# The down projection of a decoder's feed-forward layer as seven block products, its operands streamed through a ring of four slots

## The chip, the cores and the metric

The kernel runs on one core of a Trainium2 chip. The metric is the time of one execution on the device in microseconds (us), lower is better; three executions of the kernel before are given by their median. A core has five engines that run side by side, each with its own queue of instructions in program order: TensorE (PE, matrix products into the accumulators in PSUM, with its weight loads as PEld), VectorE (DVE), ScalarE (ACT), GpSimd (POOL) and SyncE (SP), which here only issues DMAs. They wait for one another through semaphores.

## The reference

One inference step of a decoder layer in float32: normalise, project, four groups of heads, output projection, then the feed-forward part that the change touches. The prompt has 1024 positions, the samples add 8, so each matrix of activations has 1032 columns when it lies transposed (features on the partitions).

```python
def conv_ffn(x, g, w_up, conv_w, conv_b, w_down, buf):
    t = x.shape[1]
    up = rmsnorm(x, g) @ w_up
    ext = jnp.concatenate([buf.astype(up.dtype), up], axis=1)
    conv = conv_b + sum(ext[:, i:i + t] * conv_w[i] for i in range(CONV_W))
    a, gate = jnp.split(conv, 2, axis=-1)
    y = (jax.nn.silu(gate) * a) @ w_down
    return y, ext[:, t:]
...
xp = xp + f.astype(xp.dtype)
```

`D_MODEL` is 1024, `D_FF` is 2816 (22 tiles of 128 features). `w_down` is 2816 x 1024: its product with the gated activations, added to the residual x, is the last stage of the kernel and the subject of this case.

## The kernel before, in words

Three things are common to all large products here. First, a float32 operand is split into a high part, which ACT makes by a copy to the type float32r, and a low part, which DVE makes by subtracting the high part from the raw value. Second, a product is three matmuls: high by high, high by low, low by high. Third, one stationary block of 128x128 weights meets some hundred columns of activations.

**The up projection** (line 1338 on, `seven`) runs in 22 passes p, one for each pair of a value tile and its gate tile. Each pass is a 2x2 block product by Winograd's scheme: seven block products P1 to P7 for eight, on sums of activations (T1 to T4) and of weights (S1 to S4), each product with 4 tiles of depth, 2 column parts of 258 and 3 matmuls per part: 168 matmuls of 258 columns in a pass. Behind it DVE and ACT put the pieces together, run the convolution over positions (`affine`, `taps`), `silu` and `gated`, and SP stores the gated tile of 1032 columns to DRAM (`scr_act`, `act_store`). `NPROD` is 154, the number of these products.

**The down projection** (PE lines 1401 to 1432, `down`) is a plain product. `GRAN` cuts it into 24 granules: a group of output tiles d and a range of depth tiles f. SP loads a granule's weights (`down_load`, line 857) into one of two buffers `dnr` when the granule two before is done, ACT splits them (`down_hi`, line 1900), DVE too (`down_low`, line 2750). The 22 tiles of activations are loaded back from DRAM once (`act_loads`, line 864), split once (ACT line 1766, DVE line 2598 by `act_hi`, `act_low`) and stay in SBUF as `fh`, `fl`, `hhi`, `hlo`. For each of the 8 output tiles d there are 22 f, 3 column parts of 344 and 3 matmuls: 8 x 22 x 3 x 3 = 1584 matmuls of 344 columns. Two sets of three PSUM banks take turns by d, so DVE adds the residual to a finished tile d (`add_y`, line 2824) while PE fills the other set. GpSimd loads the residual into `yst` and stores the sum. The last tile d is added and stored in three parts (line 2835, SP line 900).

The order on every engine is written out by hand; there is no scheduler. Line 1418 is the only wait of PE on the adds:

```python
if dd[0] >= 2 and fa_ == 0:
    pe.wait_ge(S("x2_add"), KC + dd[0] - 1)
```

Of the kernel before, what the change touches and what calls it, by code (L numbers as in the profile page):

```python
# [98 lines left out]
def build(nc, t):  # L99
# [5 lines left out]
    with ctx:  # L105
# [161 lines left out]
        fh = []  # L267
        for n, o5 in ((0, Q), (1, Q + 8256), (2, set0), (3, set0 + 8256), (4, Q + 16512), (5, Q + 24768), (6, Q + 33024),
                      (7, Q + 41280), (12, set1), (13, set1 + 8256), (14, set1 + 16512), (19, conv0), (20, conv0 + 8256),
                      (21, base)):  # L270
            h_, o6 = at(f"fh{n}", [P, COLS], f32r, o5)
            fh.append((n, h_[:, :], at(f"fl{n}", [P, COLS], f32r, o6)[0][:, :], at(f"fr{n}", [P, COLS], f32, o6)[0][:, :]))
        fh = {n: (h_, l_, r_) for n, h_, l_, r_ in fh}
        for j in range(KC):
            fh[8 + j if j < 4 else 11 + j] = (hhi[:, j, :], hlo[:, j, :], hlr[:, j, :])
        dst2 = [spare, set0 + 16512]
        dnh, dnl, dnr = [], [], []
        for n in range(2):
            h_, o6 = at(f"dnh{n}", [P, 1024], f32r, dst2[n])
            dnh.append(h_)  # L280
            dnl.append(at(f"dnl{n}", [P, 1024], f32r, o6)[0])
            dnr.append(at(f"dnr{n}", [P, 1024], f32, o6)[0])
        yst = at("yst", [P, COLS], f32, base + 8256)[0]
# [192 lines left out]
        g_end = {d: max(n for n in range(NG) if d in GRAN[n][0]) for d in range(KC)}  # L476
# [65 lines left out]
        def k_total(n):  # L542
            return 64 * (n // 4 + 1) if n < NKA else 64 * (NKA // 4) + 16 * ((n - NKA) // 4 + 1)
        SET_END = {}
# [13 lines left out]
        def _(sp):  # L558
# [2441 lines left out]
```

## Time and profile before

| what | value |
|---|---|
| median of three runs | 1352.65 us (1349.96 to 1356.93) |
| span of the profiled execution, first to last instruction | 1348.4 us |
| the same execution's own time | not recorded; the median lies 4.25 us above the span |
| PE busy | 1302.1 us (97%) |
| DVE busy | 946.2 us (70%) |
| ACT busy | 555.1 us (41%) |
| down projection, first product to the end of the last | 1092.8 to 1345.6 us |

The span is what the instructions cover; the time of a run has a few microseconds more around it. "Busy" of PE includes overlap: matmuls are pipelined, so one that lasts 0.28 us starts 0.12 us after the one before, and it is the distance of the starts that adds up. In a timeline a bracket at the row's end gives the idle time of the engine before it and what released it. PEclk is the clock that was granted to TensorE as a share of 2.4 GHz: 0.50 is 1.2 GHz.

### The profile page before, as it was taken

How to read it: one execution, taken by the hardware profiler on the slowest of the kernel's cores; microseconds unless marked ns; L12 is line 12 of the kernel's file. 1: busy time of each engine (PE TensorE's matmuls, PEld its weight loads, DVE VectorE, ACT ScalarE, POOL GpSimd, SP SyncE). 2: the span in 40 equal slices, each digit the busy share in tenths (PEclk: the TensorE clock that was granted, in tenths of full speed). 3: DMA queues.
4: the chain of work that ended last, by engine and by line, in shares of the span. 5: the costliest groups of instructions: out<-in, count | busy, mean ns of one | idle time of the engine just before them, and what ended most of it. 6: DMA issues, size and time to landing. Idle time of an engine off the chain costs nothing.

```text
span 1348.4 us, 24281 instructions
## 1 busy us (share of the span) xinstructions
PE 1302.1 (97%) x9271; PEld 1198.1 (89%) x9271; DVE 946.2 (70%) x1390; ACT 555.1 (41%) x913; POOL 217.1 (16%) x222
## 2 busy tenths in 40 slices
PE   7999999989989999999999999999999999999999
PEld 5888787767667678899999999999999998999999
DVE  6678889988898767567697888887788894211111
ACT  6623111355567665343545435445445463000100
POOL 0420034323333430100201101101101000000000
PEclk9999999979999999999999999999999999999999
DMA  9868766679999772421322222222222383322222
GB/s 304 302 208 252 208 176 182 211 225 259 295 322 354 227 224 76 148 97 62 94 88 70 96 71 71 95 71 71 96 71 71 124 302 115 106 85 81 75 75 75
DMA packets 151071, 206.82 MB, mean 153 GB/s; under 512 B 12862, under 2 KB 112728, under 8 KB 150676
## 3 DMA queue, kind: packets, MB, share of 16 engines
q1 hardware_dynamic: 133204, 146.74, 35.0%
q0 software_dynamic: 12848, 46.73, 10.9%
q10 hardware_dynamic: 4904, 11.81, 2.9%
q8 instruction: 73, 1.20, 0.4%
q14 instruction: 42, 0.34, 0.1%
HBM read 174.91 MB, written 29.82 MB: 152 GB/s over the span
## 4 chain that ended last, share of the span: by engine, by line
PE 74%; DVE 10%; DMA 5%; issue 3%; POOL 3%; SPq 3%; ACT 1%; ACTq 0%; DVEq 0%; POOLq 0%
PE ps L1349 9%; PE ps L1350 9%; PE ps L1351 9%; PE ps L1410 6%; PE ps L1411 6%; PE ps L1412 6%; PE ps L1191 4%; PE ps L1132 3%; PE ps L1134 3%; PE ps L1133 3%; PE ps L1214 2%; PE ps L1290 1%; DMA upr<-in_w_upL 1%; PE ps L1292 1%; PE ps L1291 1%
## 5 line engine op out<-in xcount | busy, mean ns | idle before, releaser
L1349 PE MATMUL ps<-hhi,uph 128*128 128x258 f32 x704 | 200.8, 285 | 1.3 <-ACT ug L1828 0.7
L1350 PE MATMUL ps<-hlo,uph 128*128 128x258 f32 x704 | 199.5, 283 | 0.0
L1351 PE MATMUL ps<-hhi,upl 128*128 128x258 f32 x704 | 199.2, 283 | 0.0
L2750 DVE TENSOR_TENSOR dnl<-dnr,dnh 128x896 fp32r<-128x896 f32 (+2 forms) x24 | 27.2, 1135 | 176.3 <-ACT dnh L1900 176.3
L1349 PEld LDWEIGHTS ps<-hhi,uph 128*128 128x128 f32 x704 | 133.9, 190 | 2.6 <-DVE ug L2708 1.4
L1350 PEld LDWEIGHTS ps<-hlo,uph 128*128 128x128 f32 x704 | 134.1, 190 | 0.0
L1351 PEld LDWEIGHTS ps<-hhi,upl 128*128 128x128 f32 x704 | 133.6, 190 | 0.0
L1132 PE MATMUL ps<-whi,hhi 128*128 128x512 f32 (+1 forms) x336 | 125.7, 374 | 0.9 <-PE ps L1134 0.6
L1134 PE MATMUL ps<-whi,hlo 128*128 128x512 f32 (+1 forms) x336 | 124.4, 370 | 0.0
L1133 PE MATMUL ps<-wlo,hhi 128*128 128x512 f32 (+1 forms) x336 | 124.0, 369 | 0.0
L1410 PE MATMUL ps<-fh,dnh 128*128 128x344 f32 x336 | 107.5, 320 | 3.2 <-DVE dnl L2750 3.2
L1411 PE MATMUL ps<-fl,dnh 128*128 128x344 f32 x336 | 107.8, 321 | 0.0
L1412 PE MATMUL ps<-fh,dnl 128*128 128x344 f32 x336 | 107.2, 319 | 0.0
L1900 ACT ACTIVATE dnh<-dnr 128x896 fp32r<-128x896 f32 (+2 forms) x24 | 23.7, 987 | 194.7 <-DMA dnr<-in_w_down 194.7
L2925 POOL TENSOR_TENSOR upr<-upr 128x512 f32<-128x512 f32 x22 | 30.8, 1398 | 447.0 <-DMA upr<-in_w_upL 447.0
L1191 PEld LDWEIGHTS ps<-vst,pts 128*128 128x128 f32 x576 | 72.3, 198 | 30.4 <-issue 27.4
L1769 ACT ACTIVATE uph<-upr 128x1024 fp32r<-128x1024 f32 (+1 forms) x66 | 79.3, 1202 | 39.6 <-DMA upr<-in_w_upL 36.1
L2628 DVE TENSOR_TENSOR upl<-upr,uph 128x1024 fp32r<-128x1024 f32 (+1 forms) x66 | 92.1, 1396 | 0.1
L1191 PE MATMUL ps<-vst,pts 128*128 128x65 f32 x576 | 79.5, 285 | 9.1 <-DVE oN L2333 7.1
L2862 POOL DMA_INDIRECT vring<-in_cache_a_v,gtab x64 | 62.3, 973 | 137.0 <-PE ps L1214 130.8
L2020 DVE TENSOR_TENSOR ring<-ring,qb 128x1024 f32<-128x1024 f32 x64 | 78.0, 1218 | 7.3 <-DMA ring<-in_cache_a_k 5.7
L2028 DVE TENSOR_REDUCE sA<-ring 128x16 f32<-128x1024 f32 x64 | 78.0, 1219 | 1.9
(357 smaller groups left out, 3567.2 us busy)
## 6 DMA issues: line engine op xcount, KB each, us to landing
upr<-in_w_upL SPq DMA_DIRECT2D x88, 256.0 KB, 3.3
ring<-in_cache_a_k SPq DMA_DIRECT2D x170, 128.0 KB
scr_act<-va SPq DMA_DIRECT2D x22, 516.0 KB, 2.6
ring<-in_cache_a_k ACTq DMA_DIRECT2D x86, 128.0 KB
wst<-in_w_in SPq DMA_DIRECT2D x32, 256.0 KB, 3.9
fr<-scr_act SPq DMA_DIRECT2D x14, 516.0 KB, 5.2
dnr<-in_w_down SPq DMA_DIRECT2D x12, 448.0 KB, 4.2
dnr<-in_w_down SPq DMA_DIRECT2D x10, 512.0 KB, 4.0
```

What stands on the lines that cost most here:

```text
L1132: pe.matmul(out, lh, whi[:, sl, 0:w], start=(kc == 0), stop=False)
L1133: pe.matmul(out, lh, wlo[:, sl, 0:w], start=False, stop=False)
L1134: i = pe.matmul(out, ll, whi[:, sl, 0:w], start=False, stop=(kc == KC - 1))
L1191: i = pe.matmul(ps[:, 6, 0:HD + 1], pts[:, g % 2, j, :], vst[:, hp % 2, j, VCOL[H % 2]], start=(j == 0), stop=(j == nb - 1))
L1349: pe.matmul(out, hi_, r_hi[:, cs], start=(first and i == 0), stop=False, skip_group_check=not first)
L1350: pe.matmul(out, hi_, r_lo[:, cs], start=False, stop=False, skip_group_check=not first)
L1351: m = pe.matmul(out, lo_, r_hi[:, cs], start=False, stop=(i == 3), skip_group_check=not first)
L1410: pe.matmul(out, hi_, a_hi[:, cs], start=first, stop=False)
L1411: pe.matmul(out, hi_, a_lo[:, cs], start=False, stop=False)
L1412: m = pe.matmul(out, lo_, a_hi[:, cs], start=False, stop=last)
L1769: act.activation(uph[p % 2][:, a:b, :], upr[p % 2][:, a:b, :], ACT.Copy).then_inc(S("st_hi"), 1)
L2628: dve.tensor_tensor(upl[p % 2][:, a:b, :], upr[p % 2][:, a:b, :], uph[p % 2][:, a:b, :].bitcast(f32), ALU.subtract).then_inc(S("st_lo"), 1)
```

## The change

The down projection takes the form that the up projection has. The output (1024 features by 1032 columns) is cut into 2x2 quarters of 512 features by 516 columns, the depth into two halves of `HK` = 11 tiles. Seven block products of 11 steps each, 77 steps `st` in all, take the place of the plain product, in the order P1, P2, P6, P7, P4, P5, P3 (`PHASE`, called phases here; steps 0 to 10 are P1, 11 to 21 P2, 22 to 32 P6, 33 to 43 P7, 44 to 54 P4, 55 to 65 P5, 66 to 76 P3). A step has 4 output tiles j, 2 column parts of 258 and 3 matmuls: 24 matmuls, 1848 in all.

- Nothing stays split. Each step's activations (`bh`, `bl`, 516 columns) and weights (`wh`, `wl`, 512 columns) are split anew into one of four slots, `st % 4`, by ACT (`b_hi`, `w_hi`) and DVE (`b_lo`, `w_lo`). `b_hi(st)` waits until PE is done with step st - 4. Weights of depth 11 to 21 come through four raw slots `wr` (`ring_load(st)`, SP, which waits for the same step); those of depth 0 to 10 stay as `w_a` and `w_b`, and are summed in place. `act_t` are 22 raw tiles of activations, summed in place too.
- 99 sums run on DVE (`down_sum`): T1 to T4 of activations, S1 to S4 and a second S2 of weights. Three tables say at which step, ahead of `b_lo`, between, or behind `w_lo`.
- All 8 PSUM banks hold the four tiles j of one quarter. P1 is copied out by ACT to `u_p1` (`p1_copy`), four copies behind `w_hi(13)`; DVE adds it to three residual quarters (x12, x22, x21; 2064 columns each). After each other phase DVE adds the banks to a residual quarter (`evict`, four adds of 516 columns), behind its work for the step three after the phase's last one, and PE waits for it at the next phase (`bank_free`). 
- The residual comes as quarters of 1.06 MB on SP (`x_quarter`), and SP stores the result. GpSimd has nothing left in this stage.

The core of the diff:

```diff
...
-        GRAN = [((0, 1), f, f + 4) for f in (0, 4, 8, 12)] + [((d,), 16, FT) for d in (0, 1)] \
-            + [((d,), a, b) for d in range(2, KC) for a, b in ((0, 8), (8, 15), (15, FT))]
-        NG = len(GRAN)
...
+        PHASE = ["P1", "P2", "P6", "P7", "P4", "P5", "P3"]
+        NSTEP = len(PHASE) * HK
...
+        for k_ in range(HK):
+            SUM_BEFORE[5 + k_ if k_ < 6 else 2 * k_ - 1].append(("T3", k_))
+            SUM_BEHIND[5 + k_ if k_ < 6 else 2 * k_ - 1].append(("T2", k_))
+            SUM_BEHIND[13 + k_].append(("S3", k_))
+            SUM_BEFORE[step_of("P6", k_) - 1].append(("S2", k_))
+            SUM_BEFORE[step_of("P7", k_)].append(("T4", k_))
+            SUM_BETWEEN[step_of("P4", k_)] += [("S1", k_), ("S2b", k_)]
+            SUM_BEFORE[step_of("P5", k_) - 2].append(("T1", k_))
+            SUM_BEFORE[step_of("P3", k_) - 1].append(("S4", k_))
+        SUM_BEHIND[26].append(("x12", 0))
+        SUM_BEHIND[34].append(("x22", 0))
+        SUM_BEHIND[38].append(("x21", 0))
...
+            def ring_load(st):
+                ph, k = PHASE[st // HK], st % HK
+                mi = 1 if ph in ("P6", "P4") else 0
+                n = RING_NO[st]
+                sp.wait_ge(S("p_done"), NPROD + st - 3)
+                sp.dma_start(wr[st % 4][:, :], down_w(mi, HK + k)).then_inc(S(f"ring_ld{n % 4}"), 16)
...
+            for st in range(HK, NSTEP):
+                ph, k = PHASE[st // HK], st % HK
+                if st in RING_NO:
+                    ring_load(st)
+                if ph == "P2":
+                    if k == 1:
+                        x_quarter(1, xq1, 0, 1)
+                    if k == 3:
+                        x_quarter(2, xq2, 1, 1)
+                    wb_load(k)
+                if st == step_of("P6", 3):
+                    for j in range(4):
+                        y_store("P2", j)
+                if st == step_of("P6", 6):
+                    sp.wait_ge(S("y_out"), 16 * 4)
+                    x_quarter(3, xq0, 1, 0)
+                if st == step_of("P5", 0):
...
-            def down(n, d, f, chs, first, last):
...
+            def bank_free(ph, j):
+                if ph == "P1":
+                    pe.wait_ge(S("c_sum"), 5 * (FT - 1) + (-1, 1, 3, 4)[j])
+                    return
+                if ph == "P2":
+                    pe.wait_ge(S("copied"), 3 * FT + j + 1)
+                    return
+                pe.wait_ge(S("x2_add"), KC + 4 * (PHASE.index(ph) - 2) + j + 1)
+            FRESH = ("P1", "P6", "P5")
+            for st in range(NSTEP):
+                ph, k = PHASE[st // HK], st % HK
+                n = st % 4
+                pe.wait_ge(S("mv_lo"), MV0 + st + 1)
+                pe.wait_ge(S("st_lo"), ST0 + st + 1)
+                fresh = ph in FRESH
+                for j in range(4):
+                    if k == 0:
+                        bank_free(ph, j)
+                    hi_, lo_ = wh[n][:, j * P:(j + 1) * P], wl[n][:, j * P:(j + 1) * P]
+                    for ch in range(2):
+                        out, cs = ps[:, 2 * bank_of[j] + ch, 0:HC], slice(ch * HC, (ch + 1) * HC)
+                        pe.matmul(out, hi_, bh[n][:, cs], start=(fresh and k == 0), stop=False, skip_group_check=not fresh)
+                        pe.matmul(out, hi_, bl[n][:, cs], start=False, stop=False, skip_group_check=not fresh)
+                        m = pe.matmul(out, lo_, bh[n][:, cs], start=False, stop=(k == HK - 1), skip_group_check=not fresh)
+                        if k == HK - 1 and (j < 3 and ch == 1 or j == 3 and ch == 0 and st == NSTEP - 1):
+                            m.then_inc(S("pair_done"), 1)
+                m.then_inc(S("p_done"), 1)
...
+            def b_hi(st):
+                ph, k = PHASE[st // HK], st % HK
+                if st < 3:
+                    act.wait_ge(S("p_done"), p_no["P3", FT - 2])
+                elif st > 3:
+                    act.wait_ge(S("p_done"), NPROD + st - 3)
...
+            def w_hi(st):
+                ph, k = PHASE[st // HK], st % HK
+                if ph in ("P1", "P2", "P4"):
+                    n = RING_NO[st]
+                    act.wait_ge(S(f"ring_ld{n % 4}"), ring_total(n))
...
+            def p1_copy(j):
+                act.wait_ge(S("pair_done"), j + 1) if j < 3 else act.wait_ge(S("p_done"), NPROD + HK)
+                b0 = 2 * (slotF, slotW, slotX, slotY)[j][FT - 1]
+                act.activation(u_p1[:, j, :].rearrange("p (b c) -> p b c", b=2), ps[:, b0:b0 + 2, 0:HC], ACT.Copy)\
+                    .then_inc(S("copied"), 1)
...
+            for st in range(4, NSTEP):
+                b_hi(st)
+                w_hi(st)
+                if st == HK + 2:
+                    for j in range(4):
+                        p1_copy(j)
...
+            def b_lo(st):
+                dve.wait_ge(S("mv_hi"), MV0 + st + 1)
+                dve.tensor_tensor(bl[st % 4][:, :], operand(st), bh[st % 4][:, :].bitcast(f32), ALU.subtract).then_inc(S("mv_lo"), 1)
...
+                if name == "S2":
+                    made("S3", k)
+                    raw = ring_landed(step_of("P6", k))
+                    summed(raw, raw, wa, ALU.subtract)
...
+            def evict(ph, j):
+                e = EVICT.index(ph)
+                end = (PHASE.index(ph) + 1) * HK
...
-            def add_y(d):
-                dve.wait_ge(S("p_done"), NPROD + g_end[d] + 1)
-                dve.wait_ge(S("y_ld"), 16 * (d + 1))
-                dve.tensor_tensor(c3(yst[:, :]), U3(d % 2), c3(yst[:, :]), ALU.add).then_inc(S("x2_add"), 1)
...
+            for st in range(4, NSTEP):
+                for name, k in SUM_BEFORE[st]:
+                    down_sum(name, k)
+                b_lo(st)
+                for name, k in SUM_BETWEEN[st]:
+                    down_sum(name, k)
+                w_lo(st)
+                for name, k in SUM_BEHIND[st]:
+                    down_sum(name, k)
+                ph = PHASE[(st - 3) // HK]
+                if (st - 3) % HK == HK - 1 and ph in EVICT:
+                    for j in range(4):
+                        evict(ph, j)
+            for j in range(4):
+                evict("P3", j)
...
```

Where the instructions now stand. First DVE around the end of the plain product's third output tile, before the change (`dnl` a granule's low weights, `yst` the residual tile, `ps` the accumulators):

```order
1306 L2750 TENSOR_TENSOR dnl_204<-dnr_205,dnh_203 128x768 [waits st_hi]
1307 L2750 TENSOR_TENSOR dnl_207<-dnr_208,dnh_206 128x768 [waits st_hi]
1308 L2750 TENSOR_TENSOR dnl_204<-dnr_205,dnh_203 128x1024 [waits st_hi]
1309 L2824 TENSOR_TENSOR yst<-ps,yst 128x1032 [waits y_ld,p_done]
1310 L2750 TENSOR_TENSOR dnl_207<-dnr_208,dnh_206 128x896 [waits st_hi]
```

One add stands between two splits, a granule ahead of PE. Next DVE after the change where P2 ends and P6 begins (`wr_213` is the ring slot of step 25, `wa_186` the third sum's operand of k = 3, `bl_206` and `wl_209` the low parts of step 24, `xq_225` the residual quarter that takes P2):

```order
1369 L2912 TENSOR_TENSOR wr_213<-wr_213,wa_186 128x512 [waits ring_ld1,s_vec]
1370 L2896 TENSOR_TENSOR bl_206<-act_163,bh_205 128x516 [waits mv_hi]
1371 L2901 TENSOR_TENSOR wl_209<-wr_208,wh_207 128x512 [waits st_hi]
1372 L2984 TENSOR_TENSOR xq_225<-ps,xq_225 128x516 [waits y_ld,pair_done]
1373 L2984 TENSOR_TENSOR xq_225<-ps,xq_225 128x516 [waits pair_done] x2
1374 L2984 TENSOR_TENSOR xq_225<-ps,xq_225 128x516 [waits p_done]
```

The four adds that empty the banks stand behind a sum that waits for a load of weights. That load is the third of these rows of SP (`wr_213`), which waits until step 21, the last of P2, is done:

```order
1089 L955 DMA wr_223<-in_w_down 128x512 [waits p_done]
1090 L955 DMA wr_208<-in_w_down 128x512 [waits p_done]
1091 L955 DMA wr_213<-in_w_down 128x512 [waits p_done]
1092 L965 DMA o_yT<-xq_225 128x516 [waits x2_add] x4
1093 L955 DMA wr_218<-in_w_down 128x512 [waits p_done]
```

Before the change SP had one load of weights for a granule here and no stores. Last, ACT where P1 ends (`bh_210` and `wh_212` belong to step 13, `u_p_228` is the copy of P1):

```order
1186 L2045 ACTIVATE wh_207<-wr_208 128x512 [waits ring_ld0]
1187 L2034 ACTIVATE bh_210<-act_174 128x516 [waits stage_ld1,p_done]
1188 L2045 ACTIVATE wh_212<-wr_213 128x512 [waits ring_ld1]
1189 L2050 ACTIVATE u_p_228<-ps 128x516 [waits pair_done] x3
1190 L2050 ACTIVATE u_p_228<-ps 128x516 [waits p_done]
```

The copies that free the banks for P2 stand behind the high part of step 13's weights, which waits for a load that SP issues when step 9 is done.

## Rows read from the trace of the kernel before

**Rows 1.** The page, first part: span and PE's busy time.

```profile
span 1348.4 us, 24281 instructions
...
PE 1302.1 (97%) x9271; PEld 1198.1 (89%) x9271; DVE 946.2 (70%) x1390; ACT 555.1 (41%) x913; POOL 217.1 (16%) x222
```

**Rows 2.** The page, second part: tenths in 40 slices of 33.7 us.

```profile
DVE  6678889988898767567697888887788894211111
...
PEclk9999999979999999999999999999999999999999
```

**Rows 3.** Windows: start:end, length, busy of each engine (count), PEclk, DMA, GB/s.

```profile
700.00:800.00 100.00, 100.00 (x834) 100.00 (x834) 80.67 (x90) 44.25 (x65) 12.99 (x10) 1.00 0.25 80
...
1200.00:1250.00 50.00, 50.00 (x321) 50.00 (x320) 6.87 (x6) 4.98 (x5) 1.59 (x3) 1.00 0.27 81
```

**Rows 4.** Timeline of PE: start, length, line, operands, count, [idle before].

```profile
1092.79 0.32 PE L1410 MATMUL ps<-fh,dnh 128*128 128x344 f32 x1
...
1130.19 0.43 PE L1410 MATMUL ps<-fh,dnh 128*128 128x344 f32 x1 [3.24 <-DVE dnl L2750]
```

**Rows 5.** Timeline of DVE at the span's end.

```profile
1345.62 0.52 DVE L2835 TENSOR_TENSOR yst<-ps,yst 128x344 f32<-128x344 f32 x1 [2.78 <-PE ps L1412]
```

**Rows 6.** Timeline of DVE in the last pass of the up projection.

```profile
1087.28 0.69 DVE L2708 TENSOR_TENSOR ug<-ps,ug 128x516 f32<-128x516 f32 x1
1088.00 0.69 DVE L2714 SCALAR_TENSOR_TENSOR ug<-ug,rstd_bc 128x516 f32<-128x516 f32 x1
1088.61 2.37 DVE L2598 TENSOR_TENSOR fl<-fr,fh 128x1032 fp32r<-128x1032 f32 x2
...
1103.58 1.23 DVE L2744 TENSOR_TENSOR va<-va,vg 128x1032 f32<-128x1032 f32 x1
```

**Rows 7.** Groups of DVE by form, 600 to 1100 us: count, busy us, mean ns.

```profile
L2628 DVE TENSOR_TENSOR upl<-upr,uph 128x1536 fp32r<-128x1536 f32 x21 | 36.8, 1752 | 0.1
...
L2704 DVE TENSOR_TENSOR ua<-ps,p1c 128x516 f32<-128x516 f32 x22 | 15.3, 696 | 2.8
...
L2598 DVE TENSOR_TENSOR hlo<-x,hhi 128x516 fp32r<-128x516 f32 x3 | 2.1, 690 | 0.0
```

**Rows 8.** Timeline of ACT: a copy of 516 columns and what follows it.

```profile
1060.63 0.58 ACT L1828 ACTIVATE u2c<-ps 128x516 f32<-128x516 f32 x1
1061.12 1.06 ACT L1769 ACTIVATE uph<-upr 128x1024 fp32r<-128x1024 f32 x1
```

**Rows 9.** Loads, issue to landing: 256 KB by SP, then 516 KB by GpSimd.

```profile
L813 SPq DMA_DIRECT2D upr<-in_w_upL x22: 539/540/653, 560.1 to 1045.7; - x22
...
DMA to landing us min/median/max: 2.9/3.1/4.4
...
L2938 POOL DMA_DIRECT2D yst<-scr_x x8: 527/528/625, 1120.3 to 1325.1; - x8
...
DMA to landing us min/median/max: 3.6/4.0/6.4
```

**Rows 10.** The chain of waits, 1085 to 1348 us, then a window of crowded DMA.

```profile
1120.13 7.67 DMA dnr<-in_w_down
...
1095.00:1100.00 5.00, 5.00 (x33) 5.00 (x33) 4.96 (x6) 3.48 (x6) 0.00 (x0) 1.00 1.03 397
```

**Rows 11.** Timeline of PE, then windows, where the granted clock falls or stays.

```profile
535.63 0.55 PE L1300 MATMUL ps<-hhi,wohi 128*128 128x256 f32 x1 [2.25 <-DVE hlo L2440]
...
455.00:460.00 5.00, 4.01 (x24) 2.10 (x24) 2.86 (x9) 2.91 (x7) 1.21 (x2) 0.66 0.64 208
530.00:535.00 5.00, 2.71 (x24) 2.46 (x22) 3.04 (x8) 4.20 (x13) 1.07 (x3) 0.97 0.00 0
535.00:540.00 5.00, 4.37 (x20) 4.40 (x21) 4.86 (x13) 1.85 (x2) 1.02 (x2) 0.50 0.25 82
540.00:545.00 5.00, 5.00 (x40) 5.00 (x39) 3.18 (x5) 1.04 (x2) 0.00 (x0) 0.84 1.02 413
1130.00:1135.00 5.00, 4.81 (x30) 4.81 (x31) 5.00 (x6) 5.00 (x6) 0.00 (x0) 1.00 0.00 0
```

More of the change, by code:

```diff
@@ L273, in build @@
[L273 to L283, printed above, removed]
+        HK = FT // 2
@@ L284, in build @@
+        xq0, o6 = at("xq0", [P, 4, H2], f32, A1 + 2 * 4128)
+        assert o6 == A2
+        xq1, o6 = at("xq1", [P, 4, H2], f32, conv0)
+        xq2, o6 = at("xq2", [P, 4, H2], f32, o6)
+        assert o6 == set1
+        u_p1, o6 = at("u_p1", [P, 4, H2], f32, rstd_off)
+        assert o6 <= cend
         ps = ctx.enter_context(nc.psum_tensor("ps", [P, 8, 512], f32))
@@ new lines, in _ @@
+                    for f in range(4):
+                        act_load(f, True)
+                    sp.wait_ge(S("p_done"), p_no["P5", FT - 1])
+                    for k in range(8):
+                        wa_load(k)
+            sp.wait_ge(S("p_done"), p_no["P2", FT - 1])
+            for f in range(4, 8):
+                act_load(f)
+            sp.wait_ge(S("p_done"), p_no["P7", FT - 1])
+            for f in range(8, 16):
+                act_load(f)
+            sp.wait_ge(S("p_done"), p_no["P3", FT - 1])
@@ L904, in build @@
+            for j in range(3):
+                y_store("P3", j)
+            for ch in range(2):
+                sp.wait_ge(S("x2_add"), KC + 24 + ch)
+                c0 = H2 + ch * HC
+                sp.dma_start(t["o_yT"][:, 3, c0:c0 + HC], xq1[:, 3, ch * HC:(ch + 1) * HC]).then_inc(S("y_out"), 16)
+            sp.wait_ge(S("out"), 48)
+            sp.wait_ge(S("y_out"), 16 * 17)
         class PassTargets:
@@ L1917, in _ @@
                         w_vec(c + 1)
+                    else:
+                        w_hi(0)
+                        w_hi(1)
                     silu(c - 1)
+                    if not more:
+                        b_hi(2)
+                        w_hi(2)
                     u3_copy(c)
@@ new lines, in evict @@
+            def evict(ph, j):
+                e = EVICT.index(ph)
+                end = (PHASE.index(ph) + 1) * HK
+                dve.wait_ge(S("pair_done"), 3 * (e + 1) + j + 1) if j < 3 else dve.wait_ge(S("p_done"), NPROD + end)
+                buf = OUT_AT[ph][0]
+                if j == 0:
+                    if ph == "P2":
+                        dve.wait_ge(S("y_ld"), 16)
+                    elif ph != "P5" and ph != "P3":
+                        made({"P6": "x12", "P7": "x22", "P4": "x21"}[ph], 0)
+                b0 = 2 * (slotF, slotW, slotX, slotY)[j][FT - 1]
+                if ph == "P3" and j == 3:
+                    dve.wait_ge(S("pair_done"), 3 * 7 + 1)
+                    for ch in range(2):
+                        if ch == 1:
+                            dve.wait_ge(S("p_done"), NPROD + end)
+                        q = buf[:, j, ch * HC:(ch + 1) * HC]
+                        dve.tensor_tensor(q, ps[:, b0 + ch, 0:HC], q, ALU.add).then_inc(S("x2_add"), 1)
+                    return
+                q = c2(buf[:, j, :])
+                dve.tensor_tensor(q, ps[:, b0:b0 + 2, 0:HC], q, ALU.add).then_inc(S("x2_add"), 1)
```

336 lines of the change are left out of this document (191 added, 145 removed).

## The prediction, made before the changed kernel ran

> **What bounds the kernel now.** I read the page's first part: PE is busy in 97% of the span [rows 1]. Then its second part: DVE is nearly idle in the last slices while PE and its clock stay high [rows 2]. So the down projection, the last fifth of the span, is bound by PE alone, and time can be won there only by giving PE less to do or by filling its gaps. The windows show its pace: 321 matmuls of 344 columns in 50 us, 0.156 us each, and in the up projection, whose form the change copies, 834 matmuls of 258 columns in 100 us, 0.1199 us each [rows 3]. The timeline of PE shows one gap in the down stage, 3.24 us before 1130.19; the first product starts at 1092.79 [rows 4], and DVE's last add starts at 1345.62, as the last product ends [rows 5]. The stage takes 1345.6 - 1092.8 = 252.8 us.
>
> **What PE has to do after.** 7 x 11 x 4 x 2 x 3 = 1848 matmuls of 258 columns. The form is that of the up projection, so I take its pace: a step of 24 is 24 x 0.1199 = 2.88 us, 77 steps are 221.6 us. Without any wait the stage would be 252.8 - 221.6 = 31.2 us shorter. The rest of this text is about what comes back.
>
> **DVE's load.** 154 splits, 99 sums, 24 adds and 3 sums of 2064 columns replace 24 + 22 splits and 10 adds. An operation of 516 columns lasts 0.69 us, from PSUM 0.70 [rows 7], but the next starts 0.61 us later if it does not need its result (1088.00 to 1088.61), 0.72 if it does (1087.28 to 1088.00) [rows 6]. In the new order neighbours are independent, so I count 0.61; at 0.70 the waits below grow by 2.1 us in all (23 operations by 0.09). The large sum: 516 columns take 690 ns and 1536 take 1752 [rows 7], which is 1.04 ns a column, so 2064 take 2.3 us, 2.2 of distance. Total: 277 x 0.61 + 3 x 2.2 = 176 us of 222 (198 us at full durations). DVE has room on the whole; the fullest phase, P4, has 4 operations a step, 2.44 us of 2.88. ACT has two copies a step, each 0.49 us from start to start [rows 8]. The question is where DVE must be on time.
>
> **The load behind which it stands.** A ring load of 256 KB is issued when step st - 4 is done. The trace has no such load of 2 KB rows; the nearest row, 256 KB in 512-byte pieces by the same queue, lands after 2.9 us at best and 4.4 at worst [rows 9]; the largest value anywhere near is 7.67 us, behind other transfers [rows 10]. From below the nearest is the last store, 172 KB, which ends with the span 2.3 us after DVE's add (1348.4 - 1346.1) [rows 1, 5]. I take 2.9, nearest in size and queue, and 0.05 for the semaphore. The Trainium skill (DMA: Bandwidth & Descriptors, "Anatomy of one DMA — SWDGE (gpsimd) path") gives a fit of about 2.0 us and the bytes over 436e3, 2.6 us for this size; by it the five waits below would sum to some 1.6 us less.
>
> **The waits of PE at a change of phase.** All 8 banks are in use, so the first step of a phase needs the banks emptied. DVE does that behind its work for the third step of the next phase. Counted from the moment the old phase ends:
> - P2 to P6: DVE's row before the splits of step 24 is the sum for step 25, and its load is issued only when step 21, the last of P2, is done. 2.95 for the load, three operations 1.83, the first add 0.69, semaphore 0.05: PE waits 5.5 us. The other three adds (0.61 apart) stay ahead of PE (0.72 a tile).
> - P5 to P3: the same with S4. 5.5 us.
> - P7 to P4: S1 of step 46 waits for that step's load, issued one step (2.88) earlier, then three operations and the add: 5.5 - 2.88 = 2.65 us.
> - P6 to P7: here DVE is behind. From the issue of step 32's load, four steps (11.5 us) before P6 ends: 2.95, then S2 and the splits of 31 to 35 with three T4, in all 14 operations (8.5), the large sum x22 (2.2), the add 0.7, together 14.4: PE waits 2.9 us.
> - P4 to P5: only T1 and splits, no load. DVE's add is ready 0.3 us early. 0.
> - P1 to P2: ACT's copies stand behind w_hi(13). SP issues the residual quarter of 1.06 MB for xq1 as soon as the first has landed, about when step 8 is done, and step 13's load behind it. GpSimd's load of half that size lands after 4.0 us [rows 9], and at 397 GB/s [rows 10] the second half adds 1.3: 5.3, with the loads around it step 13's weights land some 5 us after step 9 is done, which is 2.1 after P1 has ended; w_hi and the first copy add 1.2. PE waits 3.3 us (1.3 if the quarter does not hold the load up, 7 if it does by 3.7 more).
> - Inside P6 the sum x12 delays one step by 0.2 us.
>
> Each restart costs 0.1 (0.43 for 0.32 in [rows 4]), five times: 0.5. The sum is 5.5 + 5.5 + 2.65 + 2.9 + 3.3 + 0.2 + 0.5 = 20.6 us.
>
> **The start, the steps and the end.** Before, DVE ends `gated` at 1104.8 with two long splits ahead of it that go [rows 6]; after, it should end about 1102.7 and the splits of step 4 at 1104.0, where PE needs them at 1092.8 + 4 x 2.88 = 1104.3. I cost it at 0; the cover is 0.3 us, and the first H2 loads (T3) have about 2 us. Both together may cost 0 to 3. In P6 and P3 a step's sum, two splits: 2.95 + 1.83 + 0.1 = 4.9 us after the issue, where 5.76 are given: no wait. The end: the add of 516 columns before the last ones now overlaps the last matmuls, and two adds of 258 follow where one of 344 did (0.52, [rows 5]): 0.3 us more. GpSimd's loads go; they cost nothing before.
>
> **The clock.** [Rows 11] show what a gap can do: after a stretch with little matmul work and a gap of 2.25 us before 535.63, the granted clock is 0.50, 1.2 GHz, from about 534.7 to 541.6 (0.03, 1 and 0.32 of three windows of 5 us), of which 6.0 us lie behind the gap: 3.0 us lost. At 455 to 460 it is low for 3.4 us: 1.7 lost. After 3.24 us of gap in the down stage it stayed at 1.00. So a gap of 3 us may do no harm, one of 5.5 is beyond all that the trace shows; I take a fall for the two long ones, at the mean of the two prices, 2.35 each: 4.7 us. All five would be 11.8, none 0.
>
> **Sum.** 221.6 + 20.6 = 242.2, that is 10.6 less than 252.8; 0.3 and 4.7 back: 5.6 us less. The profiled execution's own time is not known, only its span of 1348.4, from which the median lies 4.25 us; I carry the difference over to the median: 1352.65 - 5.6 = 1347.0 us. What can be told from no change here is 0.5%, 6.8 us: below 1345.9 is faster, above 1359.4 slower.
>
> **Rivals.**
> - The clock stays up in all gaps: the 3.24 us gap speaks for it, the fall at 535 against it. 1352.65 - 10.3 = 1342.
> - Every change of phase cools the clock: 1347.0 + 3 x 2.35 = 1354. The Trainium skill (TensorE: Matmul & The Clock Gate, "HAM oscillation — how this bites in real kernels") says that a wait for DMA between groups of matmuls throttles the clock again each time; the one gap of that kind in this trace does not agree.
> - The banks are emptied in time: DVE takes the adds while the old phase's last step runs, so that only restarts, quarter and clock remain. That would need the load of step 25 to land before its issue allows; only if I misread the order. 1352.65 - 31.2 + 3 to 6: 1324 to 1328.
> - Slower: ring loads are slow, because the new stage moves 256 KB every 2.88 us with quarters and stores between. PE can go on in P6 and P3 only if a load lands within 3.8 us. At 6 us (between 4.4 and 7.67) three steps take 6 + 2 + 2.9 = 10.9 instead of 8.65, 0.75 a step over some 20 steps: 15 us; the four phase changes that hang on loads cost 3.1 more each, 12.4: 1347 + 27 = 1374. It is slower than before from a load of about 4.2 us on, and by 0.5% from 4.8. For it: 7.67. Against it: the median of 3.1 and DMA rates near 80 GB/s where the ring alone would be about 90.
>
> **Chances.** The forecast 0.40, clock up 0.17, clock down everywhere 0.18, banks in time 0.06, slow loads 0.14, the rest 0.05 for something not seen. The forecast's own range is 1341 to 1352. The range over the cases: 1337 to 1359. Faster: 0.17 from the forecast, 0.16 clock up, 0.06 banks, 0.01: 0.40. Slower: 0.13 slow loads, 0.01 clock, 0.01: 0.15. Within 0.5%: 0.45.
>
> **What would show it.** In the new timeline of PE: starts 0.12 us apart inside a step; gaps near 5.5 us at the starts of P6 and P3, near 3 at P2, P7, P4, none at P5, each released by DVE's add or ACT's copy. In the windows: clock 0.50 behind the two long gaps. In DVE's waits: idle for the ring loads in P6, P4, P3. Loads of 256 KB landing in about 2.9 us. I would be wrong if PE waits inside phases for splits, if DVE's starts are over 0.70 apart, or if the loads need over 4 us.

## The result, and the profile after

The changed kernel takes 1361.64 us (median of 20 runs, 1352.81 to 1368.18) against 1354.66 us for the kernel before (20 runs on the same chip, 1346.58 to 1360.28). The ratio is 1.0057, interval 1.0038 to 1.0075: 7.7 us slower, between 5.1 and 10.2. The forecast was 5.6 us faster.

First, the page of the changed kernel, where it answers to [rows 1, 2]:

```profile
span 1360.2 us, 25417 instructions
...
PE 1286.8 (95%) x9535; PEld 1181.0 (87%) x9535; DVE 1062.1 (78%) x1615; ACT 601.7 (44%) x1025; POOL 207.2 (15%) x207
...
DVE  7678879988988767567687787788788885687955
...
PEclk9999999969999899999899999999999997999999
```

DVE is now as full in the last fifth as elsewhere, and PEclk has a new dip there, to 7 in slice 34 (1122 to 1156 us); its lower digits in slices 9, 14 and 20 belong to the part whose code is the same. Next, the timeline of PE: the first product of the down stage and each row there with idle time before it.

```profile
1097.45 0.28 PE L1558 MATMUL ps<-bh,wh 128*128 128x258 f32 x1
...
1113.60 0.36 PE L1558 MATMUL ps<-bh,wh 128*128 128x258 f32 x1 [1.69 <-DVE wl L2901]
...
1143.12 0.55 PE L1558 MATMUL ps<-bh,wh 128*128 128x258 f32 x1 [12.14 <-ACT u_p L2050]
...
1182.07 0.55 PE L1558 MATMUL ps<-bh,wh 128*128 128x258 f32 x1 [5.39 <-DVE xq L2984]
...
1198.07 0.35 PE L1558 MATMUL ps<-bh,wh 128*128 128x258 f32 x1 [0.22 <-DVE wl L2901]
...
1218.22 0.36 PE L1558 MATMUL ps<-bh,wh 128*128 128x258 f32 x1 [2.77 <-DVE xq L2984]
...
1254.00 0.36 PE L1558 MATMUL ps<-bh,wh 128*128 128x258 f32 x1 [2.59 <-DVE xq L2984]
...
1322.57 0.55 PE L1558 MATMUL ps<-bh,wh 128*128 128x258 f32 x1 [5.33 <-DVE xq L2984]
...
1356.49 0.28 PE L1560 MATMUL ps<-bh,wl 128*128 128x258 f32 x1
```

The rows are, in order: step 5, then the starts of P2, P6, a step inside P6, P7, P4 and P3. The stage runs from 1097.45 to 1356.77 (1356.49 + 0.28), 259.3 us, where the plain product took 252.8 [rows 4, 5]. It starts 4.7 us later than in the profile before; the part ahead of it is the same code, and over the ten other profiles of kernels that share it the start lies anywhere from 1089.5 to 1101.8, so the lengths of the stage are compared and not the spans. The length grew by 6.5 us, and what follows the last product went from 2.8 us (1348.4 - 1345.6) to 3.4: 7.1 us of the 7.7.

The gaps sum to 30.1 us. PE's own work is 77 x 2.88 = 221.6; the remaining 7.6 us are restarts and a low clock. The windows of the changed kernel (columns as in [rows 3]) show the latter, beside [rows 11]:

```profile
1135.00:1140.00 5.00, 0.00 (x0) 0.00 (x0) 3.72 (x6) 1.71 (x4) 0.00 (x0) 0.50 0.96 326
1140.00:1145.00 5.00, 1.88 (x9) 1.91 (x10) 1.90 (x3) 3.14 (x7) 0.00 (x0) 0.50 0.92 301
1145.00:1150.00 5.00, 5.00 (x35) 5.00 (x35) 3.20 (x5) 1.12 (x2) 0.00 (x0) 0.77 0.32 89
1180.00:1185.00 5.00, 2.93 (x14) 2.96 (x15) 3.73 (x7) 0.63 (x1) 0.00 (x0) 0.66 0.45 168
1215.00:1220.00 5.00, 2.23 (x15) 2.05 (x14) 5.00 (x9) 1.15 (x2) 0.00 (x0) 0.90 0.00 0
1220.00:1225.00 5.00, 5.00 (x35) 5.00 (x35) 3.74 (x7) 1.16 (x2) 0.00 (x0) 0.76 0.01 3
1320.00:1325.00 5.00, 2.43 (x11) 2.46 (x12) 4.23 (x7) 0.63 (x1) 0.00 (x0) 0.64 0.35 130
1325.00:1330.00 5.00, 5.00 (x32) 5.00 (x31) 0.00 (x0) 0.64 (x1) 0.00 (x0) 0.68 0.36 128
```

A window of 5 us at 0.68 has been at 1.2 GHz for 3.2 us (twice 0.32 of 5). The clock fell around four of the gaps, those before P2, P6, P7 and P3. Behind the gaps it was low for about 4.2, 2.8, 3.4 and 5.6 us of running work, half of which is lost: 8 us, against 7.6 with restarts from the balance.

**Why PE waited 12 us for P2.** P1 ended at 1130.98. ACT's timeline of the changed kernel shows what its copies stood behind:

```profile
1134.41 0.63 ACT L2045 ACTIVATE wh<-wr 128x512 fp32r<-128x512 f32 x1 [11.32 <-DMA wr<-in_w_down]
...
1141.86 0.63 ACT L2045 ACTIVATE wh<-wr 128x512 fp32r<-128x512 f32 x1 [5.02 <-DMA wr<-in_w_down]
1142.39 2.06 ACT L2050 ACTIVATE u_p<-ps 128x516 f32<-128x516 f32 x4
```

The first row is `w_hi(11)`, the second `w_hi(13)`, the weights of step 13. SP's timeline shows when their load, the L955 row at 1134.70, was issued:

```profile
1114.23 11.07 SPq L935 DMA_DIRECT2D act<-scr_act  x10
1125.41 0.36 SPq L925 DMA_DIRECT2D act<-scr_act  x1
1125.87 0.38 SPq L935 DMA_DIRECT2D act<-scr_act  x1
1126.30 0.43 SPq L960 DMA_DIRECT2D xq<-scr_x  x1
1126.78 0.62 SPq L955 DMA_DIRECT2D wr<-in_w_down  x1
...
1133.73 0.38 SPq L960 DMA_DIRECT2D xq<-scr_x  x1
...
1134.70 0.43 SPq L955 DMA_DIRECT2D wr<-in_w_down  x1
```

Step 9 was done at 1097.45 + 10 x 2.88 + 1.69 = 1127.9. But SP was still behind its own queue: the second halves of the activations, at most four in flight, kept it until 1126.3; the first residual quarter left only then and took 7.4 us to 1133.7; the second quarter and step 13's load stood behind it, and the load took 7.1 more. SP does not only keep the order here, it stands still: `x_quarter` makes it wait until the quarter before has landed, and everything behind it in the queue waits too.

```python
def x_quarter(i, dst, mi, ni):
    if i:
        sp.wait_ge(S("y_ld"), 16 * i)
    sp.dma_start(dst[:, :, :], xq(mi, ni)).then_inc(S("y_ld"), 16)
```

So step 13's load left 6.8 us after its own condition (step 9 done) was met, and the wait that held it back is one for a load, on the queue that issues loads. Landings (issue to landing, least, median, most) of those second halves:

```profile
L935 SPq DMA_DIRECT2D act<-scr_act x18: 319/427/1324, 1108.0 to 1125.9; - x18
...
DMA to landing us min/median/max: 3.2/4.1/6.0
```

and over the whole span, from the page's sixth part:

```profile
wr<-in_w_down SPq DMA_DIRECT2D x44, 256.0 KB, 2.7
...
act<-scr_act SPq DMA_DIRECT2D x36, 258.0 KB, 4.0
```

A ring load alone lands in 2.5 to 3.0 us, mostly near 2.6; nearly the same size with three others of its queue in flight in 4.1. The gap at step 5 comes from the first reader of these activations: DVE's timeline has the first T3 waiting for its load, and the splits of step 5 behind it.

```profile
1107.98 0.69 DVE L2901 TENSOR_TENSOR wl<-wa,wh 128x512 fp32r<-128x512 f32 x1
1111.55 0.69 DVE L2912 TENSOR_TENSOR act<-act,act 128x516 f32<-128x516 f32 x1 [2.88 <-DMA act<-scr_act]
```

**Why PE waited 5.4 us for P6.** P2 ended at 1176.68 (1182.07 - 5.39). DVE's timeline of the changed kernel has the sum for step 25 waiting for its load, the two splits of step 24 and then the four adds:

```profile
1179.42 0.69 DVE L2912 TENSOR_TENSOR wr<-wr,wa 128x512 f32<-128x512 f32 x1 [0.24 <-DMA wr<-in_w_down]
1180.03 0.69 DVE L2896 TENSOR_TENSOR bl<-act,bh 128x516 fp32r<-128x516 f32 x1
1180.63 0.68 DVE L2901 TENSOR_TENSOR wl<-wr,wh 128x512 fp32r<-128x512 f32 x1
1181.23 2.50 DVE L2984 TENSOR_TENSOR xq<-ps,xq 128x516 f32<-128x516 f32 x4
```

### The profile page after: what moved, and what is told of

It reads as the page before. It is cut to its first block, busy times and chain, and to the rows that moved or that the text cites. A ratio compares the mean times of both kernels' runs of the same rounds, so it can differ in the third digit from the quotient of the medians.

```text
span 1360.2 us, 25417 instructions
## 1 busy us (share of the span) xinstructions
PE 1286.8 (95%) x9535; PEld 1181.0 (87%) x9535; DVE 1062.1 (78%) x1615; ACT 601.7 (44%) x1025; POOL 207.2 (15%) x207
## 4 chain that ended last, share of the span: by engine, by line
PE 67%; DVE 13%; DMA 8%; issue 4%; SPq 3%; POOL 3%; ACT 1%; ACTq 1%; POOLq 0%; DVEq 0%
PE ps L1482 8%; PE ps L1483 8%; PE ps L1484 8%; PE ps L1558 5%; PE ps L1560 4%; PE ps L1559 4%; PE ps L1324 4%; PE ps L1265 3%; PE ps L1267 3%; PE ps L1266 3%; DMA upr<-in_w_upL 2%; PE ps L1347 2%; DMA wr<-in_w_down 1%; PE ps L1305 1%; DMA act<-scr_act 1%
## 5 line engine op out<-in xcount | busy, mean ns | idle before, releaser
L1558 PE MATMUL ps<-bh,wh 128*128 128x258 f32 x616 | 179.0, 291 | 30.1 <-DVE xq L2984 16.1
L1559 PE MATMUL ps<-bl,wh 128*128 128x258 f32 x616 | 176.5, 287 | 0.0
L1560 PE MATMUL ps<-bh,wl 128*128 128x258 f32 x616 | 175.9, 285 | 0.0
L1558 PEld LDWEIGHTS ps<-bh,wh 128*128 128x128 f32 x616 | 119.3, 194 | 31.4 <-issue 29.5
L1560 PEld LDWEIGHTS ps<-bh,wl 128*128 128x128 f32 x616 | 120.3, 195 | 0.0
L1559 PEld LDWEIGHTS ps<-bl,wh 128*128 128x128 f32 x616 | 120.1, 195 | 0.0
```

Source lines behind the costliest of these rows:

```text
L1558: pe.matmul(out, hi_, bh[n][:, cs], start=(fresh and k == 0), stop=False, skip_group_check=not fresh)
L1559: pe.matmul(out, hi_, bl[n][:, cs], start=False, stop=False, skip_group_check=not fresh)
L1560: m = pe.matmul(out, lo_, bh[n][:, cs], start=False, stop=(k == HK - 1), skip_group_check=not fresh)
```

## The experiments

Two theories stood. A: the time is lost where hand-written queues put work that frees something behind work that waits for a load (adds behind sums on DVE, copies behind `w_hi` on ACT), and each such place can be mended alone. B: the DMA engines cannot deliver in time what the stage asks, so a mended place only hands its wait on. The lengths of the down stage below run from its first product to the end of its last, in the profiled execution; medians are compared with the kernel before on the same chip (1356.41 us for adds_early, quarters_late, sum_moved and all_in, 1352.69 for t_late and best3, 1352.86 for the others). The changed kernel's 20 runs spread over 15 us, so a kernel with one run is read by its gaps and not by its time.

**adds_early.** The adds that empty the banks go ahead of the sums of the same step.

```diff
             for st in range(4, NSTEP):
+                ph = PHASE[(st - 3) // HK]
+                if (st - 3) % HK == HK - 1 and ph in EVICT:
+                    for j in range(4):
+                        evict(ph, j)
                 for name, k in SUM_BEFORE[st]:
                     down_sum(name, k)
...
-                ph = PHASE[(st - 3) // HK]
-                if (st - 3) % HK == HK - 1 and ph in EVICT:
-                    for j in range(4):
-                        evict(ph, j)
```

> The changed kernel with DVE's four adds of a phase put ahead of its work for the step three after the phase's last one, instead of behind it. Theory A (the adds are late only because they stand behind a sum that waits for a ring load, or, at P7, behind DVE's backlog): the gaps of PE at P6 (5.39 us), P7 (2.77), P4 (2.59) and P3 (5.33) fall below 0.3 each, 16.1 us in all, and with them the falls of the clock there, which I read as 6.0 us; the 12.1 us at P2 stay. The time falls by 22 us, to about 1340, faster than before the change. Rival B (DVE is simply too full: 78% busy): the wait moves inside the phases, PE waits for splits of steps 23 to 25, 34 to 36 and so on by 3 us or more each time, and at most half of the 22 us comes back, 1350.

Median 1350.58 us, ratio 0.9963 (0.9927 to 0.9999); stage 247.1 us. The gaps fell to 3.50 (P6), 1.07 (P7), 0 (P4) and 2.62 (P3). No step inside a phase waited longer than 0.23 for splits, step 5 apart, so DVE is not too full, as rival B had it; that the time came out near B's 1350 is chance. Theory A's mechanism holds, but it counted on 22 us and some 13 came back (ratio 1.0057 to 0.9963). The rest at P6 and P3 has the same cause one step earlier: DVE's timeline of this kernel shows the sum of step 24 in the work of step 23, still ahead of the adds.

```profile
1182.09 0.69 DVE L2912 TENSOR_TENSOR wr<-wr,wa 128x512 f32<-128x512 f32 x1
1182.69 0.69 DVE L2896 TENSOR_TENSOR bl<-act,bh 128x516 fp32r<-128x516 f32 x1
1183.30 0.69 DVE L2901 TENSOR_TENSOR wl<-wr,wh 128x512 fp32r<-128x512 f32 x1
1183.90 0.69 DVE L2912 TENSOR_TENSOR wa<-wa,wb 128x512 f32<-128x512 f32 x1
1184.50 2.50 DVE L2984 TENSOR_TENSOR xq<-ps,xq 128x516 f32<-128x516 f32 x4
```

P2 ended at 1181.84 (1185.34 - 3.50), so the load of step 24 was issued 2.88 us before, and 2.95 + 4 x 0.61 + 0.69 + 0.05 - 2.88 = 3.25 against 3.50. At P3, where one operation fewer stands between, it is 2.64 against 2.62. In this profile step 5 waited 3.71 and P2 8.92.

**quarters_late.** The three residual quarters are loaded at steps 15, 17 and 19, no longer at the stage's head, 12 and 14.

```diff
-            x_quarter(0, xq0, 0, 0)
             for st in range(HK, NSTEP):
...
-                    if k == 1:
+                    if k == 4:
+                        x_quarter(0, xq0, 0, 0)
+                    if k == 6:
                         x_quarter(1, xq1, 0, 1)
-                    if k == 3:
+                    if k == 8:
                         x_quarter(2, xq2, 1, 1)
```

> The changed kernel with the three residual quarters of 1.06 MB issued at steps 15, 17 and 19 instead of ahead of step 11, at 12 and at 14. Theory A (two quarters stand ahead of step 13's weights in SP's queue and in the DMA rings): that load lands near 1132 on the clock of the profile instead of 1141.8, the gap of PE at P2 falls from 12.1 to about 2.5 us, the clock may still fall once, the time is 10 us less: 1352. Rival B (the raw activations hold the weights up, since SP ends their issue only at 1126.2): the gap stays above 8 us and the time within 4 us of the changed kernel.

Median 1356.87 us, ratio 0.9993 (0.9965 to 1.0021); stage 256.1 us; the gap at P2 6.30, that at step 5 2.97. This lies between the two theories. The two profiles can be laid side by side: SP issued the last load of the reload at 1126.19 (1125.87 in the changed kernel) and P1 ended at 1130.96 (1130.98). SP's timeline has step 13's load, then ACT's the first split that needed it:

```profile
1128.50 0.43 SPq L955 DMA_DIRECT2D wr<-in_w_down  x1
...
1135.99 0.63 ACT L2046 ACTIVATE wh<-wr 128x512 fp32r<-128x512 f32 x1 [0.19 <-DMA wr<-in_w_down]
```

The load now left 0.4 us after step 9 was done and no longer 6.8: nearly half of the 12.1 us was thus SP held by the quarters. But it still took 7.4 us to land, with the end of the reload and the loads of steps 11 and 12 and of `wb` issued shortly ahead of it: the rest is mostly this crowding.

**sum_moved.** The S2 of step 25 and the S4 of step 69 (k = 3), whose loads are issued at the end of P2 and P5, move one step back, behind the adds.

```diff
-            SUM_BEFORE[step_of("P6", k_) - 1].append(("S2", k_))
+            SUM_BEFORE[step_of("P6", k_) - (k_ != 3)].append(("S2", k_))
...
-            SUM_BEFORE[step_of("P3", k_) - 1].append(("S4", k_))
+            SUM_BEFORE[step_of("P3", k_) - (k_ != 3)].append(("S4", k_))
```

> The changed kernel with two of 99 sums moved by one place: the sum of S2 for step 25 and of S4 for step 69 stand ahead of the splits of steps 25 and 69 and no longer of 24 and 68; nothing else changes. Theory A (that one wait for a load makes the gaps at P6 and P3): both fall from 5.4 us to below 0.5, while those at P7 (2.8) and P4 (2.6) stay. Rival B (the adds themselves or DVE's load make them): they shrink by the one operation, 0.6 us, to 4.7.

One run, 1364.77 us. The gaps: 4.35 at P6, 4.26 at P3. The sum for step 24 takes over; it stands six distances of 0.61 ahead of the adds (DVE starts it at 1178.32 and them at 1181.95), and 2.95 + 6 x 0.61 + 0.69 + 0.05 - 2.88 = 4.5. The gaps came out near B's 4.7, but one place fewer on DVE would not explain the 1.0 us that they lost, and the sum before does; theory A had overlooked it. To take away one wait for a load uncovers the one of the step before.

**x22_late.** The large sum x22 (2064 columns) moves from behind step 34 to behind step 36: `SUM_BEHIND[34]` becomes `SUM_BEHIND[36]`.

> The changed kernel with the one sum of 2064 columns (x22) behind step 36 instead of 34, that is behind the adds of P6 and no longer ahead of them. Theory A (DVE's backlog makes the gap at P7, and the large sum is 2.2 us of it): the gap at P7 falls from 2.77 to 0.6 us, all other gaps stay. Rival B (DVE waits there for something of PE, so that its work is hidden): the gap stays above 2 us.

One run, 1357.11 us. P7's gap went from 2.77 to 0.61, by 2.16, as theory A has it:

```profile
1214.79 0.36 PE L1558 MATMUL ps<-bh,wh 128*128 128x258 f32 x1 [0.61 <-DVE xq L2984]
```

DVE's timeline of the changed kernel has the sum itself, 2.22 us from its start to that of its neighbour, and the usual distance of 0.61 ahead of it:

```profile
1209.72 0.69 DVE L2912 TENSOR_TENSOR act<-act,act 128x516 f32<-128x516 f32 x1
1210.33 0.69 DVE L2896 TENSOR_TENSOR bl<-act,bh 128x516 fp32r<-128x516 f32 x1
...
1213.35 2.31 DVE L2912 TENSOR_TENSOR xq<-xq,u_p 128x2064 f32<-128x2064 f32 x1
1215.57 0.69 DVE L2912 TENSOR_TENSOR act<-act,act 128x516 f32<-128x516 f32 x1
```

**copies_early.** ACT's four copies of P1 go ahead of the high parts of step 13.

```diff
+                if st == HK + 2:
+                    for j in range(4):
+                        p1_copy(j)
                 b_hi(st)
                 w_hi(st)
-                if st == HK + 2:
-                    for j in range(4):
-                        p1_copy(j)
```

> The changed kernel with ACT's four copies of P1 one step earlier in its order: ahead of b_hi(13) and w_hi(13), behind w_hi(12); nothing else changes. Theory A (PE waits at P2 for a copy that stands behind a load): in the changed kernel w_hi(12) started at 1135.7, 4.7 us after P1's end at 1131.0, and w_hi(13) at 1141.9. So the gap falls from 12.1 to about 5.9 us; then step 13, whose weights land as late as before, 10.9 us after P1's end, has PE wait about 2 us more inside P2. Rival B (PE waits for P2's own weights, the copy is only the last to arrive): the gap stays above 9 us.

One run, 1352.89 us, beside 1352.86 before; stage 254.7 us. P2 waited 3.02, step 5 4.37. What is left at P2 is `w_hi(12)`, which the copies still follow. Not all of the 9.1 us is the edit's: SP reached the first quarter 7.6 us before P1's end here and 4.7 before it in the changed kernel, as the start of the stage and the gap at step 5 shifted. In this same profile `w_hi(13)` started at 1138.08; copies behind it would have let P2 start near 1139.3 in place of 1134.73, so the edit is worth some 4.6 us. Theory A holds, the copies waited for a load that PE did not need yet. And because SP was earlier here, step 13's weights were in time and the 2 us expected inside P2 did not come.

**t_late.** T3 and T2 move two steps back (`SUM_BEFORE[5 + k_ ...]` becomes `SUM_BEFORE[7 + k_ ...]`, `SUM_BEHIND` likewise).

> The changed kernel with the sums T3 and T2 two steps later in DVE's order (T3 of k = 0 ahead of step 7's splits instead of step 5's); nothing else changes. In the five profiles that keep the loads as they are, the gap of PE at step 5 and that at P2 vary (1.7 and 12.1, 3.7 and 8.9, 2.5 and 10.9, 3.3 and 9.2) but their sum stays at 12.4 to 13.8 us. Theory A (the landing of the weights for step 13 sets when P2 starts, whatever PE does before): the gap at step 5 goes to 0 and the one at P2 grows to 12 to 14 us, the time does not change. Rival B (two separate losses): the first goes, the second stays at 9 to 12, and the time falls by 2 to 4 us.

One run, 1366.16 us. Step 5 did not wait, as expected, and P2 waited longer than the 12 to 14 us expected:

```profile
1146.52 0.55 PE L1558 MATMUL ps<-bh,wh 128*128 128x258 f32 x1 [16.18 <-ACT u_p L2050]
```

In this profile SP issued the first quarter at 1128.82, 2.5 us later than in the changed kernel, and step 13's load took 8.0 us. That is theory A in kind: the landing of step 13's weights sets the start of P2, and what is spared at step 5 is paid there; nothing of B's 2 to 4 us came back. Why the reload was slower here was not looked into; profiles of one kernel each don't settle 2 us of it.

**deeper.** Seven second halves of the activations in flight for four: the semaphore's `i % 4` becomes `i % 7`, and SP waits for the load seven before.

> The changed kernel with the second halves of the activations (18 loads of 258 KB) seven in flight instead of four. Theory A (the DMA engines' rate bounds this stretch: they are busy for 0.92 to 1.00 of it): SP is done issuing earlier, but each load takes longer, 5 to 6 us, step 13's weights land at most 2 us earlier, the gap at P2 is 10 to 12 us and the 1.7 us at step 5 stay within 1 us. Rival B (the number in flight bounds it: 4 x 258 KB in 4.0 us are 264 GB/s): the loads keep their 4 us, all land some 6 us earlier, and the gap at P2 falls to 6 us.

One run, 1353.07 us; stage 258.5 us. P2 waited 6.84 for 12.1, but step 5 waited 2.96, and the clock fell in six places for four, so that the stage gained only 0.9 us. A load now took longer:

```profile
DMA to landing us min/median/max: 3.1/5.8/6.8
```

7 x 258 KB in 5.8 us is 311 KB/us, 4 x 258 in 4.1 is 252. So neither theory holds alone. By these quotients the limit of four cost a fifth of this queue's rate; from its first issue to its last landing the reload took 20.1 us for 23.0, an eighth less. And with seven the transfers crowd each other: the first quarter took 8.6 us to land for 7.4.

**all_in.** adds_early, quarters_late, copies_early, x22_late and t_late together, and a part of the reload behind the first ring loads:

```diff
-            for f in H2_ORDER[7:-1]:
+            for f in H2_ORDER[7:12]:
                 act_load2(f)
-            sp.wait_ge(S("act_st"), 16 * FT)
-            act_load(21)
-            act_load2(21)
...
+                if st == HK:
+                    for f in H2_ORDER[12:14]:
+                        act_load2(f)
...
```

(The next two follow at step 12, the last ones at step 13.)

> All cures together: adds early, quarters at steps 15, 17 and 19, the raw activations for T3 of k = 8 to 10 and tile 21 issued behind the ring loads of steps 11, 12 and 13, ACT's copies of P1 ahead of its work for step 13, T3 and T2 two steps later, x22 two steps later. Theory A: all gaps of PE in the down stage fall below 0.5 us each and the clock stays at 2.4 GHz; the stage takes 222 to 226 us instead of 260.4 and the time is 35 us less than the changed kernel's, 1326. Rival B (the chip's rate for small loads bounds the first two phases whatever the order): 5 us or more of waits remain between steps 5 and 22, 1335.

Median 1335.47 us, ratio 0.9829 (0.9785 to 0.9874); stage 238.2 us. Three long waits are left: 4.45 at P2 (copies behind `w_hi(12)`), 3.54 at P6 and 2.54 at P3 (adds behind the sum of the step before). Theory A missed these second places. B's figures came true (1335, and 5.0 us of waits up to step 21), but not its reason: best2 asks the same loads of the chip and has no wait at P2.

**best2.** all_in, with adds and copies one step earlier still (`st - 3` becomes `st - 2`, `HK + 2` becomes `HK + 1`), and S3 with its loads of `wb` three steps later.

> All cures, one step further than in all_in: adds ahead of DVE's work for the step two (not three) after the phase's last, the copies of P1 ahead of ACT's work for step 12, and the loads of w_b and the sums S3 three steps later. Theory A (in all_in the adds at P6 and P3 stood behind the sum for step e + 3, in the work for e + 2, whose load is issued when step e - 1 is done; the copies stood behind w_hi(12)): the gaps at P6 (3.5 us) and P3 (2.5) go to 0, that at P2 (4.4) to about 1.5, the clock falls at most once. The stage takes 224 to 228 us and the time is 10 us below all_in's, 1325. Rival B (the adds now hold up the splits of steps e + 2, which PE needs 2.9 us after the phase's end, and the wait only moves there): at P6 and P3 gaps of 1 to 3 us one or two steps later, 1331 or more.

Median 1327.44 us, ratio 0.9812 (0.9783 to 0.9841); stage 227.8 us (1093.95 to 1321.78). None is left at P2 or P3; P6 waited 1.13, and the others are waits for splits, the longest at steps 21 and 27. The waits of PE in the stage (us in total, times, longest), and the windows:

```profile
PE ps L1568 <- DVE wl L2911: 4.3, 6, 1.2
PE ps L1568 <- DVE xq L2994: 1.1, 1, 1.1
```

```profile
1085.00:1135.00 50.00, 49.29 (x411) 48.91 (x411) 40.38 (x61) 22.59 (x41) 0.00 (x0) 1.00 0.91 303
1135.00:1185.00 50.00, 45.49 (x373) 44.52 (x372) 40.10 (x63) 18.51 (x32) 0.00 (x0) 1.00 0.66 226
1185.00:1285.00 100.00, 99.58 (x835) 99.37 (x835) 82.83 (x130) 40.03 (x70) 0.00 (x0) 1.00 0.14 44
```

The DMA engines carry as much as in the changed kernel, which has 0.93 and 308 GB/s over 1080 to 1145 (best2 0.91 and 306), but PE waits only 5.4 us in all, at most 1.24 at a time, and the clock stays at 2.4 GHz. 227.8 - 5.4 = 222.4 us is PE's own pace, predicted as 221.6. The stage is 25.0 us shorter than the plain product's 252.8, and so is the median by 25.4.

**best3.** best2 with seven loads in flight and the quarters one step later.

> The version best2 with the second halves of the activations seven in flight instead of four and the residual quarters one step later (16, 18, 20). In best2 PE still waited 5.5 us, of which 4.0 at steps 20 to 23, for splits of weights that landed late or were summed late. Theory A (those loads queue behind a residual quarter): the gaps at steps 20 to 23 change by 1 us at most in either direction and the time stays within 2 us of best2's, 1326 to 1329. Rival B (the stretch is bound by the number of loads in flight): 3 us less.

Median 1325.87 us, ratio 0.9788 (0.9749 to 0.9826); the intervals of best2 and best3 overlap, so the two are not told apart, and neither are the two theories. The waits came to 5.0 us for 5.4; they lie at steps 21 to 23 and 27, not at 20 to 23 as was written. Both beat the kernel before by some 26 us.

## Why the prediction was wrong, step by step

- **PE's work** (2.88 us a step): right. best2 gives 222.4 us for 221.6.
- **DVE's spacing** (0.61): right. The rows under x22_late show it. Behind step 5 no step waited for splits beyond 0.22 us.
- **P6, P3, P7, P4, P5, x12**: predicted 5.5, 5.5, 2.9, 2.65, 0, 0.2; measured 5.39, 5.33, 2.77, 2.59, 0, 0.22. The mechanism, adds behind a sum that waits for a load, at P7 behind DVE's backlog, is shown by the rows of P6 above and by adds_early and x22_late, which moved the gaps of P6, P7, P4 and P3; what adds_early and sum_moved left at P6 and P3 is the same sum taken from the step before.
- **P1 to P2**: this step failed. The place was right (ACT's copies behind `w_hi(13)`), the size not: 3.3 us with an upper bound of 7, measured 12.1. The prediction let the first quarter land at the end of step 8, which is 1125.1 on the clock of the profile after, so at 5.3 us a quarter it had to leave at 1119.8. It left at 1126.3, 6.5 us late, because the reload of activations stood ahead of it on SP, at most four loads in flight; the term never counted that queue. It took 7.4 us for 5.3, 2.1 more, though the prediction quotes 7.67 for a load in that stretch [rows 10]. From there to the landing of step 13's weights it was 8.1 us for the 7.8 implied, 0.3 more. Together 8.9, against 8.8 too little in the forecast. quarters_late shows that SP held by the quarters was 5.8 us of the gap, copies_early that the place of the copies was some 4.6 in its profile; the cures overlap and do not add up.
- **The start**: costed at 0, with 0 to 3 as its bounds; 1.7 measured, between 2.5 and 4.4 in the six other kernels with the same order there. The first T3 waited for its load, as the rows above show for the changed kernel.
- **Ring loads** (2.9, median): right, mostly near 2.6 where they go alone. The Trainium skill (DMA: Bandwidth & Descriptors, "Anatomy of one DMA — SWDGE (gpsimd) path") gives 2.6 for this size, on another path of issue; the trace agrees with it for a load alone, and has 7.1 where others are in flight.
- **The clock**: two falls at 2.35, 4.7 us, were forecast; four fell, 7.6 us with restarts where 5.2 stood. Only the short gap at P4 (2.59) and that of step 5 did no harm.
- **The end**: 0.3 forecast, 0.6 measured.

The balance: gaps 30.1 for 20.1, which is 8.8 at P2, 1.7 at the start and -0.5 elsewhere; clock and restarts 2.4 more; the end 0.3 more. 12.7 us on top of -5.6 is 7.1 slower, as the profiles have it. P2's 8.8 us alone turn the forecast from 5.6 faster to 3.2 slower. The rival "slow ring loads" named the crowding, but looked for it in P6 and P3, where the loads were on time; the one crowded place is the first 50 us of the stage.

## What to carry to other kernels

Where a queue is written by hand, put what frees a buffer or a bank ahead of anything that waits for a load, and look one step further back, since the load before is next in line. That holds for the queue that issues loads too: a load that waits for another's landing holds up all loads behind it. When you cost a load, follow its issuing queue from the last point at which you know its time, with every transfer that stands ahead of it: a landing time from an empty stretch says nothing about a crowded one. A change of form and its schedule are two things: best2 issues the same instructions as the changed kernel in another order, and is some 33 us faster (ratio 0.9812 for 1.0057).

## What the runs showed of the hardware

- **Crowding of DMA.** 256 to 258 KB landed in 2.5 to 3.0 us alone, mostly near 2.6, 4.1 (median) with four of the queue in flight and 5.8 with seven; the quarters of 1.06 MB took 5.4 to 7.4 in the changed kernel.
- **The clock.** In the down stage of all twelve kernels each gap of 4.2 us or more had a stretch at 1.2 GHz around it or behind it. Between 2.5 and 3.8 us it went both ways: 2.77 (P7, changed kernel) fell, 2.59 (P4) did not; adds_early's 3.71 and 3.50 fell, quarters_late's 2.97 and the kernel before's 3.24 did not. Gaps up to 1.7 us never did. The Trainium skill (TensorE: Matmul & The Clock Gate, "HAM oscillation — how this bites in real kernels") tells of a kernel that waits about 3 to 5 us for DMA between groups of matmuls and loses its clock each time. The gaps above 4.2 us agree; 3.24, which kept it, does not.
- **DVE.** Independent neighbours of 516 columns start 0.61 us apart, though each lasts 0.69; a dependent one starts 0.72 later [rows 6].
